# A fused mLSTM and pooling layer on one core: copies, loads and waits put in another order

## The reference

```python
parts_x = _split_proj((_rmsnorm(x, norm_w) * (1 + scale) + shift) @ in_w)      # q k v o z_m gates p z_p g_branch
h_x, _, _ = _bi_mlstm(qx, kx, vx, lix, lfx, st_f, st_b)                         # both directions, chunks of 128
y_m = _mlstm_branch(h_x, parts_x, head_norm_w, branch_m_w)                      # norm per head, gated, @ branch_m_w
y_p = _pool_branch(parts_x, (rows, GRID_W), (1, 2), pool_w, pool_scale, branch_p_w)
x = x + gate * _merge(parts_x, y_m, y_p, out_w)                                 # sigmoid gates, @ out_w
return _rmsnorm(x, final_norm_w)
```

## Time and profile before

| | |
|---|---|
| median of 3 runs | 2367.08 us (2363.56 to 2370.36) |
| the profiled execution | 2371.05 us, its span 2369.2 us |
| busy: PE, DVE, ACT, POOL | 2250.3, 1545.0, 992.4, 651.1 us |
| block 2 to block 3 | the barrier is passed at about 991.6 us |
| block 3 to block 4 | at about 1840 us |

### The profile page before, as it was taken

The page is one execution under the profiler, slowest core; times in us unless marked ns, Lnnn a source line. Parts: engine busy times, 40 slices in busy tenths (PEclk is TensorE's granted clock), DMA queues, the critical chain, the costliest instruction groups (busy, mean ns, idle before and its releaser), DMA issues.

```text
span 2369.2 us, 35117 instructions
## 1 busy us (share of the span) xinstructions
PE 2250.3 (95%) x12107; PEld 1907.1 (80%) x12107; DVE 1545.0 (65%) x2616; ACT 992.4 (42%) x2022; POOL 651.1 (27%) x558
## 2 busy tenths in 40 slices
PE   7799999998999999899999998999999798999998
PEld 5588888786778888778888887888888687888878
DVE  5554567757466675466877685888877455656564
ACT  6323345435233333334444444444544535352532
POOL 0233444533333443222322321232222112020200
PEclk9899999999999999999999999999999999999999
DMA  9466688767466765568777779877678665747562
GB/s 277 144 157 165 186 234 255 224 145 227 122 184 177 203 175 131 176 204 264 246 237 252 259 240 318 267 262 244 217 261 276 197 200 160 240 157 233 178 206 98
DMA packets 405442, 497.46 MB, mean 210 GB/s; under 512 B 25832, under 2 KB 291604, under 8 KB 400788
## 3 DMA queue, kind: packets, MB, share of 16 engines
q1 hardware_dynamic: 334740, 377.76, 48.3%
q10 hardware_dynamic: 62688, 83.90, 14.5%
q0 software_dynamic: 7840, 33.56, 4.9%
HBM read 348.63 MB, written 159.07 MB: 214 GB/s over the span
## 4 chain that ended last, share of the span: by engine, by line
PE 39%; DVE 7%; ACT 4%; issue 4%; DMA 3%; SPq 1%; DVEq 0%; POOL 0%; ACTq 0%
PE bank L1926 18%; PE bank L2550 9%; PE bank L1884 3%; PE bank L2605 3%; PE bank L1897 3%; PE bank L1905 2%; PE bank L1874 1%; ACT junk_h L2665 1%; ACT hsum L2675 1%; DMA v_t<-vk_d 1%; DVE state L2093 1%; DVE wl L2789 1%; DVE wl L2098 1%; DVE yt L2806 1%; ACT wh L2657 1%
## 5 line engine op out<-in xcount | busy, mean ns | idle before, releaser
L1926 PE MATMUL bank<-xlate,wh 128*128 128x512 f32 x1536 | 512.2, 405 | 6.9 <-DVE v_t L2070 4.9
L1031 PE MATMUL bank<-xlate,wh 128*128 128x512 f32 x1280 | 410.0, 396 | 5.8 <-DVE wl L1308 3.8
L1926 PEld LDWEIGHTS bank<-xlate,wh 128*128 128x128 f32 x1536 | 279.8, 190 | 56.7 <-DVE v_t L2070 5.3
L1031 PE MATMUL bank<-xtop,wh 128*128 128x512 f32 x960 | 307.1, 397 | 7.7 <-ACT wh L1083 4.0
L1926 PE MATMUL bank<-xlate,wl 128*128 128x512 f32 x768 | 310.8, 405 | 0.0
L1031 PEld LDWEIGHTS bank<-xlate,wh 128*128 128x128 f32 x1280 | 239.1, 189 | 59.1 <-issue 7.0
L1031 PE MATMUL bank<-xlate,wl 128*128 128x512 f32 x640 | 251.5, 393 | 0.0
L1031 PEld LDWEIGHTS bank<-xtop,wh 128*128 128x128 f32 x960 | 178.3, 189 | 47.1 <-ACT wh L1083 7.6
L1336 DVE SCALAR_TENSOR_TENSOR tmp<-bank,psum 128x512 f32<-128x512 f32 x144 | 99.1, 688 | 146.4 <-PE bank L1031 106.0
L1031 PE MATMUL bank<-xtop,wl 128*128 128x512 f32 x480 | 189.2, 394 | 0.0
L1926 PEld LDWEIGHTS bank<-xlate,wl 128*128 128x128 f32 x768 | 145.9, 190 | 24.5
(11 more groups left out here) (332 smaller groups left out, 5314.8 us busy)
## 6 DMA issues: line engine op xcount, KB each, us to landing
v_t<-vk_d SPq DMA_DIRECT2D x144, 384.0 KB, 3.8
qk_d<-os SPq DMA_DIRECT2D x32, 1024.0 KB, 5.0
q_t<-qk_d SPq DMA_DIRECT2D x128, 256.0 KB, 4.1
wraw<-wpair_d ACTq DMA_DIRECT2D x23, 1024.0 KB, 7.1
rawb<-in_in_w_dram ACTq DMA_DIRECT2D x80, 256.0 KB, 5.6
wraw<-in_in_w_dram ACTq DMA_DIRECT2D x76, 256.0 KB, 4.1
vk_d<-os SPq DMA_DIRECT2D x16, 1024.0 KB, 4.5
k_t<-qk_d SPq DMA_DIRECT2D x64, 256.0 KB, 4.7
```

The lines of the kernel that those rows point to most:

```text
L1031: mm = pe.matmul(dst[:, :], a[:, kd, :], x_block(part, XB[name])[:, kd], start=(kd == 0 and n == 0), stop=(kd == KH - 1 and n == 2))
L1926: mm = pe.matmul(bank[m % 2][:, :], a[:, u % 2, k, :], xlate[part][:, BLOCK_OF[k // KH, tq], k % KH], start=(k == 0 and n == 0), stop=(k = ...
```

## The change

Four places are changed.

1. Before the barrier of block 2, SP waits for all but the last store of each slot of `gp_d`; POOL waits for the last ones at the start of block 3, ahead of its first memset.
2. `early_quarter` takes its eight loads in two halves of four, in slots 66 and 67 for quarter 0 and 68 and 69 for quarter 1, and stands behind the stores of the slot and not ahead of them.
3. In the output slots, `mix_h` (and `mix_l` on POOL) of group 2 moves from slot 3 to slot 2 and that of group 3 from slot 4 to slot 3, behind `normalise` and ahead of `squares`; SP's loads stay where they are. `gate_hidden` of slot 6 moves ahead of `residual`. In pooled slot 2, `out_stats` moves behind `gate_pooled` and `gate_hidden`.
4. In quarter 0, the last `y_l` is made on DVE and not on POOL.

```diff
@@ -584,7 +584,7 @@
             v_hi = sem2("v_hi"); v_lo = sem2("v_lo"); tz_made = sem2("tz_made"); z_made = sem2("z_made"); outer_made = sem2("outer_made")
             os_stored = [sem2(f"os_stored{n}") for n in range(2)]; kt_stored = [sem2(f"kt_stored{n}") for n in range(2)]
             ctx_stored = sem2("ctx_stored")
-            s_stored = {which: sem2(f"s_stored_{which}") for which in ("C22", "C11", "C21", "C12")}
+            s_stored = s_stored_2 = {which: sem(f"s_stored_{which}") for which in ("C22", "C11", "C21", "C12")}
             st_loaded = [sem2(f"st_loaded{n}") for n in range(NST // 2)]
             rb_hi = sem2("rb_hi"); rb_lo = sem2("rb_lo")
             l_loaded = [sem2(f"l_loaded{n}") for n in range(2)]
@@ -887,8 +887,9 @@
                     sp.wait_ge(os_stored[n], 16 * nstore[-1])
                     sp.wait_ge(kt_stored[n], 16 * nkstore[-1])
                 sp.wait_ge(ctx_stored, 16 * 3 * HEADS)
+
                 for which in S_AT:
-                    sp.wait_ge(s_stored[which], 16 * npool[-1])
+                    sp.wait_ge(s_stored[which], 16 * (npool[-1] - 1))
                 sp.wait_ge(cols_st, 32)
                 sp.wait_ge(negm_st, 16 * 2 * HEADS)
 
@@ -1786,10 +1787,10 @@
                     sp.wait_ge(h_stored[f % 2], 16 * (f // 2 + 1))
                     sp.dma_start(hother[:, l % 2, :], h_d[latent_chunk(l), :, h * HD:(h + 1) * HD]).then_inc(h_back[l % 2], 16)
 
-                def early_quarter(tq):
+                def early_quarter(tq, part_of):
 
                     sp.wait_ge(piece_done, max(m for m in range(PHALF) if PIECES[m][4] == tq) + 1)
-                    for j in range(KT // 2):
+                    for j in range(KT // 4 * part_of, KT // 4 * (part_of + 1)):
                         for part in range(2):
                             kd = 2 * j % KH
                             sp.dma_start(f32(xlate[part][:, BLOCK_OF[2 * j // KH, tq], kd:kd + 2]),
@@ -1822,9 +1823,6 @@
                         score_keys(j + KS)
                     if NHALF <= j + 3 < NL:
                         load_scores(j + 3)
-                    for tq in range(2):
-                        if t == quarter_at[tq]:
-                            early_quarter(tq)
                     if j % NCHAIN == 1 and j // NCHAIN + 1 < NX:
                         maxima(j // NCHAIN + 1)
                     if j < NHALF:
@@ -1835,6 +1833,9 @@
                         store_h(j - 1)
                     if NHALF <= j + 1 < NL:
                         other_direction(j + 1)
+                    for tq in range(2):
+                        if t - quarter_at[tq] in (0, 1):
+                            early_quarter(tq, t - quarter_at[tq])
                     if t == HEAD_AT:
 
                         sp.wait_ge(s_done, NHALF)
@@ -2211,6 +2212,9 @@
                     turns[0] += 1
                     pool.wait_ge(step_done, NCS - 8 + turns[0])
 
+
+                for which in S_AT:
+                    pool.wait_ge(s_stored_2[which], 16 * npool[-1])
                 pool.memset(state[:, :, :, :], 0.0).then_inc(state_zero, 1)
                 pool.memset(cmask[:, :, :], 0.0).then_inc(mask_made, 1)
                 pool.wait_ge(mask_made, 1)
@@ -2394,7 +2398,7 @@
 
 
 
-            SPLIT = {0: 0, 1: 1, 3: 2, 4: 3}
+            SPLIT = {0: 0, 1: 1, 2: 2, 3: 3}
             GROUP = {1: 0, 2: 1, 4: 2, 5: 3}
             NORM = {1: 0, 2: 1, 3: 2, 4: 3}
             TURN_O = {5: 0, 7: 1}
@@ -2759,12 +2763,15 @@
                         else:
                             n = t - T_O
                             if i + 1 < NTQ:
-                                if n in SPLIT:
+                                if n in (0, 1):
                                     pooled_hi(i + 1, SPLIT[n])
                                 if n in GROUP:
                                     branch_hi(i + 1, GROUP[n])
                                 if n - 1 in NORM:
                                     normalise(i + 1, NORM[n - 1])
+                                if n in (2, 3):
+
+                                    pooled_hi(i + 1, SPLIT[n])
                                 if n in NORM:
                                     squares(i + 1, NORM[n])
                                 if n - 1 in TURN_O:
@@ -2927,16 +2934,22 @@
                                 gate_hidden(0, t)
                                 if t + 1 < QT:
                                     norms(0, t + 1)
+                                else:
+
+                                    dve.wait_ge(y_hi, QT)
+                                    dve.wait_ge(y_made, QT)
+                                    dve.tensor_tensor(y_l[:, :, t * P:(t + 1) * P], yt[:, :, :],
+                                                      f32(y_h[:, :, t * P:(t + 1) * P]), ALU.subtract).then_inc(y_lo, 1)
                             else:
                                 if t == 0:
                                     residual(i - 1, KT - 1)
                                     gate_hidden(i, 1)
-                                if t == 2:
-                                    out_stats(i - 1)
                                 gate_pooled(i, 2 * t)
                                 gate_pooled(i, 2 * t + 1)
                                 if t in TURN_P:
                                     gate_hidden(i, TURN_P[t])
+                                if t == 2:
+                                    out_stats(i - 1)
                         elif t < T_O:
                             n = t - M0
                             if i == 0 and n == 0:
@@ -2948,6 +2961,8 @@
                                 out_norm(i - 1, n)
                         else:
                             n = t - T_O
+                            if i + 1 < NTQ and n - 1 in TURN_O:
+                                gate_hidden(i + 1, TURN_O[n - 1])
                             if n >= 1:
                                 residual(i, n - 1)
                             if i + 1 < NTQ:
@@ -2955,8 +2970,6 @@
                                     branch(i + 1, GROUP[n])
                                 if n in NORM:
                                     norms(i + 1, NORM[n])
-                                if n - 1 in TURN_O:
-                                    gate_hidden(i + 1, TURN_O[n - 1])
                 i = NTQ - 1
                 for q in range(2):
                     tail_stats(q)
@@ -2983,14 +2996,16 @@
                     pool.wait_ge(yp_hi, i * PG + g + 1)
                     pool.tensor_tensor(yp_l[:, g], ypt[:, :], f32(yp_h[:, g]), ALU.subtract).then_inc(yp_lo, 1)
 
-                for q in range(QT):
+                for q in range(QT - 1):
                     hidden_lo(0, q)
                 for i in range(1, NTQ):
                     for n in range(KT):
-                        if n in SPLIT:
+                        if n in (0, 1):
                             pooled_lo(i, SPLIT[n])
                         if n in GROUP:
                             branch_lo(i, GROUP[n])
+                        if n in (2, 3):
+                            pooled_lo(i, SPLIT[n])
                         if n - 1 in TURN_O:
                             hidden_lo(i, TURN_O[n - 1])
                     hidden_lo(i, 1)
```

## The result

The changed kernel takes 2383.15 us (median of 5 runs, 2380.78 to 2385.66), the kernel before 2367.08 (5 runs, 2363.56 to 2370.36). The ratio is 1.007, 95% interval 1.0055 to 1.0084: 16.1 us slower. The forecast was 2382.0. The total is right; its parts are less so, as the profile shows.

What follows compares the result with a forecast made beforehand. PE was taken as the bound, busy 2250.3 of 2369.2 us, leaving 119 us idle and some low-clock stretches. Terms -1.4 - 7.5 - 1.1 - 2.5 + 26 + 1.7 = +15.2 gave 2386 profiled, 2382 median; range 2370 to 2391.

Steps and rivals of the forecast that it cites:

- The output slots: Block 4, slots 2 to 4: moved copies wait for their loads, delaying squares; 8.7 us per quarter, +26 us in three.
- rival A: Output slots: ACT and DVE make up the 10 us before PE's unit 7, only gains remain; median 2351, chance 0.07.
- The clock: Output slots: more PE idle time brings one more stretch of lower clock in all; +1.7 us, between 0 and 5.1.
- The early loads: Block 3, slots 66 to 70: stores ahead of loads end ACT's wait; -7.5 us of 10.95 lost, 3.5 stays.
- rival C: Block 3: PE waits for xlate as long as behind ACT, so 7.5 us are not won; median 2390, chance 0.12.
- The barrier: Barrier behind block 2: without SP's wait for the last gate store, block 3 starts earlier; -1.4 us, between 0 and -1.8.
- y_l: End of quarter 0's pooled slots: DVE makes the last y_l in 1.23 us, POOL took 2.36; -1.1 us.
- out_stats: Pooled slots: 0.83 us of DVE work no longer stands ahead of the gate_pooled PE waits for; -2.5 us in three quarters.
- yt: Output slots: yt ahead of residual starts at 2104.37 and not 2105.70, shortening the chain; -1.3 us a quarter.

Runs made afterwards that it cites:

- e1: The kernel before with only the copies mix_h and mix_l of groups 2 and 3 moved a slot earlier; 2400.46 us, ratio 1.0130.
- e2: The changed kernel with the copies of groups 2 and 3 back in slots 3 and 4, all other edits kept; 2360.09 us, ratio 0.9949.
- e9: The changed kernel with only group 2's copy a slot sooner, group 3's back in slot 4; 2366.97 us, ratio 0.9990.
- e10: The changed kernel with only group 3's copy a slot sooner, group 2's back ahead of the scaling in slot 3; 2374.98 us, ratio 1.0022.
- e3: The changed kernel with the loads of mixt and zpt for groups 2 and 3 also an output slot earlier; 2355.92 us, ratio 0.9936.

## Why the prediction was right

- **The output slots (+26), right.** The waits came as written: 3.18 us in slot 2 (forecast 2.7), 6.67 in slot 3 (6), splits 12.3 us apart (over 12). Loads of 5.8 and 5.4 us (5.37). e1, e2, e9 and e10 put the cost on these two waits. The copies cost the changed kernel 27.8 us in block 4; forecast were 30 for the delay and 1.7 for the clock. That the chain has no cover (against rival A) held: the new waits in slots 2 and 3 are 30.5 us in the three quarters (3.1 to 3.5 and 6.7 to 7.2 each), and the block is longer by 27.8. One thing was read wrongly: the delay was to come out at `turn_hidden` ahead of unit 7. PE's waits for `yt` are gone (5.3 us in block 4 before), and it comes out at `og` of `residual`, 22.2 us in nine waits.
- **The clock (+1.7), mis-sized, and its overlap with the waits missed.** PE is busy 13.6 us more in block 4, outside even the 5.1 of the range. But its idle time rose by only 11.0, where the terms of block 4 gave 22. In the output slots its waits rose by 4.7 us a quarter, where 8 were forecast (for `og`, the groups and `yt` together 28.1 us in block 4, before 14.1). The step that failed is that clock and waiting were added. The chain of ACT, DVE and SP sets the time of these slots. While PE runs at 0.82, a mix of its two levels of 2.4 and 1.2 GHz, its units last longer within the same delay, and it waits less. The two stretches of 9.21 us above show it. Only behind the last wait of a quarter does the lower clock add time (26.9 and 28.0 us above). How much of the 13.6 is of either kind was not worked out.
- **The early loads (-7.5), failed in size: 2.0 in the profile.** The gain was to be the loss of 10.95 less 3.5 for the bytes. What stays of the loss is 9.0 us, and the step of slot 70 starts 28.2 us after that of slot 67, where 22 to 23 were forecast. The mechanism was half right: ACT's wait is gone and the bytes are late next, as written. Wrong was the step that turned the bytes into a time: the last load should land near 1461, when PE wants it at 1458.4. That asked only for the last load. The bytes already stop PE at the third pair, 12 matmuls into the quarter, and the 7.17 us lost there are not made up. This is rival C, and it deserved more than 0.12: it took 5.5 of the 7.5 us.
- **The barrier (-1.4)** measured 1.75, **y_l (-1.1)** 1.2. For **out_stats (-2.5)**, PE's waits for `hsum` in block 4 fall from 9.4 to 7.2 us, and by 2.6 in the mean of the five and the nine profiles.
- **yt (-1.3 a quarter)** is 1 us where the chain is late, as in the changed kernel, by the difference of e1 and e2.
- **The sum.** The terms as measured make -1.8 - 2.0 + 24.6 = +20.8 of the profiled pair. The span grew by 14.7. The other 6.1 lie outside the places changed: 4.05 ahead of the barrier (the same weight split of ACT near the end of block 2 starts at 973.40 in the one and at 969.35 in the other), 1.5 in the first slots of block 3, where the kernel before ran at a clock of 0.96 over 43 us and the changed one at 1.00, and the rest in steps below 0.6. Between the first load of block 3 and its first step on the state lie 60.2 to 62.2 us in the fourteen profiles, with both barriers alike; so much these slots vary between executions. By the medians the edits beside the copies gain 10.1 (forecast 16.4), the copies cost 26 (31.7 with the clock), and the two errors of 5 to 6 us cancel. So the total was right partly by luck.

## What to carry to other kernels

When a copy moves up in an engine's list, its load has to move with it: read for each operation moved when its input is issued and how long such a load takes behind what is queued, and if the engine's list is part of a chain that goes round, nearly every microsecond of the wait counts (27.8 of 30.5 here). With its loads moved too, the changed kernel (e3) is faster than both. In a stretch that held more bytes than it could take, no order of the loads tried here helped by more than 5 us, while leaving half of their bytes out took nearly all of the loss away; the wait that was removed came back at an early consumer, not at the last. And idle time and a lower clock are not separate terms where another engine sets the pace.

## What the runs showed that was not expected

- Two loads of 256 KB behind 1 MB in the same queue took 5.4 and 5.8 us. The Trainium skill (DMA: Bandwidth & Descriptors, section on the anatomy of one DMA) has a fit, for DMAs that GpSimd issues, that gives 2.6 for each by itself. The nearest row here is a load of 256 KB (`gt` from `gm_d`) of the changed kernel, with nothing issued on SP's queue in the 6 us before it: 3.0 us, as the quickest of its 32.
- The same list of block 2 ended 4.05 us sooner in one profiled execution than in the other, and the first matmul of block 3 lies between 983.3 and 992.0 us in the profiles of this study. A term of a few us can't be read from the end of one profile, but can from the length of the stretch it is in: the halves gave 38.95 to 39.66 us in seven profiles.
